# RWKV scan: the decayed state is formed on GpSimd and VectorE instead of by an identity product, and the outputs and the first tile are arranged anew

## What is computed

```
def step(S, inp):                       # S is (heads, 64 values, 64 keys)
    rt, wt, kt, vt, kkt, at = inp
    sa = einsum("bhvk,bhk->bhv", S, -kkt)
    S = S * wt[..., None, :] + sa[..., None] * (kkt * at)[..., None, :] + vt[..., None] * kt[..., None, :]
    return S, einsum("bhvk,bhk->bhv", S, rt)

decay = exp(-exp(-softplus(-lw) - 0.5)) ; a = sigmoid(a0 + (xa @ a1) @ a2)
kk = k * kvec[0] ; kk = kk / max(sqrt(sum(kk * kk)), 1e-12)
k  = k * (1 + (a - 1) * kvec[1])
y  = head_layernorm(y, lnx[0], lnx[1]) ; bonus = sum(r * k * kvec[2]) * v
out = ((y + bonus) * g) @ w_o
```

## Time and profile before

| | us |
|---|---|
| median of 3 runs | 3209.08 (3206.1 to 3211.09) |
| the profiled execution | 3212.0, of which the span of its trace 3210.0 |
| TensorE matmul busy | 3044.9 (95%) |
| VectorE busy | 1132.0 (35%) |
| ScalarE busy | 586.4 (18%) |
| GpSimd busy | 230.5 (7%) |

### The profile page before, as it was taken

One profiled execution on the slowest core, in us unless ns is written; L12 is line 12 of the kernel. 1 busy time (PEld: TensorE's weight loads), 2 busy tenths in 40 slices (PEclk: granted clock), 3 DMA queues, 4 the chain that ended last, 5 costly groups with the idle time before them and its releaser, 6 DMA issues. The chain is left out here.

```text
span 3210.0 us, 54308 instructions
## 1 busy us (share of the span) xinstructions
PE 3044.9 (95%) x24038; PEld 1845.4 (57%) x24038; DVE 1132.0 (35%) x2357; ACT 586.4 (18%) x1323; POOL 230.5 (7%) x202
## 2 busy tenths in 40 slices
PE   7999999899999999989987999999999799998998
PEld 5899884633333333344766444444554687887887
DVE  3455006201100110033065444421231776864650
ACT  1011013300000000022044200000111555442100
POOL 0000000100000000000022100000000323230000
PEclk9999999899999999989988999999999899998999
DMA  9846539489998899932001322333321100005430
GB/s 376 315 173 234 196 142 372 199 355 380 390 372 346 354 380 385 402 125 79 1 2 81 142 106 79 118 131 118 118 76 50 35 15 27 15 3 198 144 144 13
DMA packets 88492, 577.03 MB, mean 180 GB/s; under 512 B 9536, under 2 KB 15936, under 8 KB 20672
## 3 DMA queue, kind: packets, MB, share of 16 engines
q1 hardware_dynamic: 84800, 568.27, 45.3%
q10 hardware_dynamic: 3456, 5.24, 0.4%
HBM read 567.19 MB, written 6.29 MB: 179 GB/s over the span
## 5 line engine op out<-in xcount | busy, mean ns | idle before, releaser
L272 PE MATMUL ps<-H,ring 128*128 128x256 f32 (+1 forms) x2480 | 803.6, 486 | 12.6 <-PEq L3300 4.1
L272 PEld LDWEIGHTS ps<-H,ring 128*128 128x128 f32 x2480 | 477.8, 194 | 336.8 <-issue 296.6
L272 PE MATMUL ps<-W,ring 128*128 128x256 f32 (+1 forms) x1616 | 490.5, 465 | 9.1 <-DVE W L3133 4.1
L1962 PE MATMUL ps<-ring,W 128*32 128x512 f32 (+1 forms) x2816 | 461.4, 594 | 1.7 <-ACT H L2021 1.7
L272 PEld LDWEIGHTS ps<-W,ring 128*128 128x128 f32 x1616 | 307.1, 191 | 192.1 <-issue 166.8
L1962 PEld LDWEIGHTS ps<-ring,W 128*32 128x32 f32 (+1 forms) x2816 | 142.5, 123 | 306.7 <-issue 304.1
L1985 PE MATMUL ps<-ring,W 128*64 128x512 f32 (+1 forms) x1408 | 231.1, 594 | 0.0
L2252 DVE SCALAR_TENSOR_TENSOR W<-ps,vec,W 128x189 f32<-128x189 f32 (+3 forms) x396 | 173.2, 437 | 14.0
L3700 POOL TENSOR_TENSOR ring<-ring 128x512 f32<-128x512 f32 x96 | 131.4, 1388 | 417.6 <-DVE ring L3724 334.7
L1985 PEld LDWEIGHTS ps<-ring,W 128*64 128x64 f32 (+1 forms) x1408 | 70.9, 123 | 156.9 <-issue 156.9
L2070 DVE TENSOR_TENSOR H<-ps,H 128x256 f32<-128x256 f32 x66 | 28.0, 425 | 303.2 <-ACT H L2012 303.2
(11 more groups left out here) (464 smaller groups left out, 3173.4 us busy)
## 6 DMA issues: line engine op xcount, KB each, us to landing
ring<-weights SPq DMA_DIRECT2D x528, 1024.0 KB, 8.0
rkv<-W ACTq DMA_DIRECT2D x16, 256.0 KB, 2.0
ring<-rkv SPq DMA_DIRECT2D x8, 512.0 KB, 3.7
X<-tokens SPq DMA_DIRECT2D x2, 1024.0 KB, 9.0
ring<-rw_tiles SPq DMA_DIRECT2D x8, 256.0 KB, 2.6
rkv<-W ACTq DMA_DIRECT2D x8, 128.0 KB, 5.5
ring<-rkv SPq DMA_DIRECT2D x8, 128.0 KB, 4.0
out<-X SPq DMA_DIRECT2D x8, 128.0 KB, 1.9
```

Of the source, the lines that this page charges most:

```text
L272: mm = pe.matmul(out(o), lhsT=k.ring[:, k.slot(at), p * P:(p + 1) * P], rhs=rhs(kk), start=kk == 0 and not (shared_bank and o % 2), stop=k ...
L1962: mm = pe.matmul(ps[at:at + n, r, :], lhsT=moe.Hg[:, kt, FIRST * e + first:FIRST * e + first + n], rhs=w[e][:, kk * WIDE:(kk + 1) * WIDE], ...
```

## The change

In the recurrence, the identity product is gone. GpSimd forms `kept` = state times decay in SBUF, and VectorE computes product in PSUM times decay plus `kept`, in two instructions (one for each z), where it had one multiplication. The first product into U now starts the accumulation.

```
@@ TensorE, step_a and step_b
                 hat = sc.hat[i % 2]
-                if i < 7:
-                    for z, h in both:
-                        pe.matmul(ps[half(h), sc.U[z], 0:CH], lhsT=k.ident[half(h), half(h)], rhs=hat[half(h), z, :],
-                                  start=True, stop=False, skip_group_check=True)
...
-                                  rhs=sc.Vt[s % 2][rows, b, half(h)], start=i == 0, stop=False, skip_group_check=True)
+                                  rhs=sc.Vt[s % 2][rows, b, half(h)], start=True, stop=False, skip_group_check=True)
@@ GpSimd
+            def kept(s, i):
+
+                if 0 <= s < TILES:
+                    pool.wait_ge(sem["hat"], 7 * s + i)
+                    if i == 1:
+                        pool.wait_ge(sem["exp"], 8 * s + 8)
+                    pool.tensor_tensor(sc.kept[i % 2], sc.hat[i % 2], sc.decay(s, i).unsqueeze(2).to_broadcast([P, 2, CH]),
+                                       ALU.mult).then_inc(sem["kept"], 1)
...
+            for j in range(TILES + 1):
+                s, here = j - 1, inside(j)
+                if here:
+                    masked(j, 0, 0)
+                kept(s, 1)
+                if here:
+                    masked(j, 0, 1)
+                    masked(j, 1, 0)
+                kept(s, 2)
+                if here:
+                    masked(j, 1, 1)
+                    masked(j, 2, 0)
+                    masked(j, 2, 1)
+                for l in range(1, 5):
+                    kept(s, 2 + l)
+                    if here and l < 4:
+                        for z in range(2):
+                            masked(j, 2 + l, z)
@@ VectorE, next_state
-                    a, b = sc.chunk(0, i), 8 + sc.chunk(1, i + 1)
-                    g = sc.G[s % 2][:, a:b + 1:b - a].unsqueeze(2).to_broadcast([P, 2, CH])
-                    dve.tensor_tensor(sc.hat[(i + 1) % 2], ps[:, sc.U[0]:sc.U[1] + 1, 0:CH], g, ALU.mult).then_inc(sem["hat"], 1)
...
+                    dve.wait_ge(sem["kept"], 6 * s + i)
+                    for z in range(2):
+                        ins = dve.scalar_tensor_tensor(sc.hat[(i + 1) % 2][:, z, :], ps[:, sc.U[z], 0:CH], sc.decay(s, i)[:, z:z + 1],
+                                                       sc.kept[i % 2][:, z, :], ALU.mult, ALU.add)
+                    ins.then_inc(sem["hat"], 1)
```

```
@@ VectorE, the turn
                 next_state(s, 0)
-                if inside(q - 1):
-                    gated_output(q - 1)
-                if behind:
-                    dve.wait_ge(sem["mean"], q + 1)
...
                 next_state(s, 2)
                 if here:
                     first_inverse(j, 1)
+                if inside(q - 1):
+                    finished_output(q - 1)
+                if behind:
+                    dve.wait_ge(sem["mean"], q + 1)
...
-                    if behind and l == 5:
-                        scaled_output(q)
```

```
@@ stage_rwkv_project, SyncE
             refill(k, sp, unit_done, 14, ahead=14)
+            sp.wait_ge(k.mm.sem, k.mm.at(out_done[last[1]]))
+            sp.dma_start(first_low(k), k.a["rw_tiles"][0]).then_inc(k.low_in[0], 16)
@@ stage_rwkv
+    LOW_BANK = ((2, 0, 1), (2, 2, 2))
...
                 if i == 0:
-                    pe.wait_ge(tile_in[n % 2], 48 * (n // 2 + 1))
+                    pe.wait_ge(k.low_in[n % 2], 16 * (n // 2 + 1))
...
-                else:
+                elif n:
                     pe.wait_ge(sem["sigmoid"], 3 * n + i)
-                pe.matmul(ps[:, 2, :], lhsT=wj[:, 128 * i:128 * i + 128], rhs=TW if i else TA, start=True, stop=True).then_inc(sem["low"], 1)
+                pe.matmul(ps[:, LOW_BANK[n > 0][i], :], lhsT=wj[:, 128 * i:128 * i + 128], rhs=TW if i else TA, start=True, stop=True).then_inc(sem["low"], 1)
...
+            for z in range(2):
+                scan(0, z)
+            key_to_product(0)
+            unit_keys(0)
+            negative_keys(0)
+            decayed_a(0, 0)
+            bonus(0)
+            decayed_b(0, 0)
```

More of the change, by code:

```diff
@@ L3208, in __init__ @@
         self.BKR = two(lambda: w(1024).rearrange("p (h z i n) -> p h z i n", h=2, z=2, i=2))
-        self.G = two(lambda: w(16))
+        self.wj = [w(512), r(512)]
+        assert self.wj[0].shape == first_low(k).shape and pools["W"][1] == LOW + 512
+        self.G = [k.sm[:, 16 * n:16 * n + 16] for n in range(2)]
         self.sa = two(lambda: w(P))
-        self.hat = two(lambda: w(P).rearrange("p (z v) -> p z v", z=2))
-        self.sq, self.sqd, self.tk = w(512), w(256), k.X[:, 6:8, CTX]
+        self.hat, self.kept = (two(lambda: w(P).rearrange("p (z v) -> p z v", z=2)) for _ in range(2))
+        self.sq, self.sqd, self.tk = r(512), w(256), k.X[:, 6:8, CTX]
         self.g = [*(k.H[:, n, CTX] for n in range(3)), w(S)]
@@ L3533, in state_keys @@
                 mm.then_inc(sem["wt"], 1)
-            for j in range(-1, TILES + 2):
+            for i in range(3):
+                low(0, i)
+            key_squares(0)
+            gate(0)
+            bonus(0)
+            for j in range(TILES + 2):
                 s, q, n = j - 1, j - 2, j + 1
@@ L3689, in _ @@
         def _(pool):
[L3690 to L3701 removed]
+            pool.wait_ge(sem["masks_in"], 16)
```

139 lines of the change are left out of this document (85 added, 54 removed).

## The result

The changed kernel takes 3190.15 us in the median of six runs (3186.36 to 3192.03), the kernel before on the same chip 3208.17. The ratio is 0.9942, with a 95% interval of 0.9929 to 0.9954: 18.6 us by the ratio, 18.0 by the medians. The forecast was 3187.7, in a range of 3174 to 3199.

What follows compares the result with a forecast made beforehand. The prediction took TensorE's stream to bound the scan, with gaps made by another engine. Its terms, -10 - 5.3 - 16.3 + 8.0 + 2.2 = -21.4 us, took the median from 3209.1 to 3187.7 us, range 3174 to 3199.

Steps and rivals of the forecast that it cites:

- C: Outputs leave their places at the tile's end and before the transposes, in tiles 2 to 7: -16.3 us, -13 to -17.
- D: Added GpSimd products, port holds, VectorE half steps and a crowded level 1: +8.0 us, between +3 and +12.
- A: First tile: the first Gram product starts 10.7 us earlier, at 2495.1; counted as -10 us, between -8 and -11.
- B: Identity product gone: -4.5 us at levels 1 to 3 of six tiles, -0.8 past tile 7; together -5.3.
- +2.5 at level 1: Moved outputs overrun VectorE's idle 4.93 us at level 1, meeting GpSimd masks: 0.5 us in each of five tiles.
- the rival in which three do and the wait goes on into the next level: Outputs not hidden at level 1: 6.8 us of VectorE work into 4.93 idle, following level late; 3198 us, chance 0.12.
- three places: Where port holds lie on the path; priced: ahead of the second masking, 3.1 us, and level 4's reciprocal, 2.4 with half steps.
- 0.45 x 7: Hold of VectorE by `kept` ahead of the second masking, 0.45 us in each of seven tiles: 3.1 us.
- E: Last turn but two: outputs between steps 2 and 3, 3.7 us where VectorE idles 1.46: +2.2 us, 0 to +3.
- The slower case: GpSimd's products hold VectorE 1.04 us on the path in all 42 steps: 43.7 us, giving 3226 us; chance 0.04.

Runs made afterwards that it cites:

- the kernel with neither: The changed kernel without the identity product and without `kept`, the new state being product times decay in one instruction: 3182.58 us, 0.9923.
- the best order: The changed kernel with query products before the first masking, old places for the last outputs, bonus factor at level 3: 3180.70 us; with identity product instead of `kept`, 3187.45.

## Why the prediction was right

**The sum** was -21.4 us; the medians say -18.0, the two traces -19.7 for the scan. Every term has its counterpart, but two of them, in C and in D, agree better in size than in place.

**A, the first tile: -10.** Right, step by step. Counted from the issue of the keys, the square was to come after about 4.4 us and came after 4.35, the root was to end after 7.8 and ended after 7.7, and the first Gram product was to start after 15.5 and started after 15.4. The part alone gave 8.3. What the sum lacked is tile 0, 1.3 us longer at the lower clock.

**B, the identity product: -4.5 in the tiles.** Measured between the kernel with and the one without it: -3.4 in the tiles, of 12.5 us of instructions. Levels 1 to 3, where the forecast put the whole gain, give 3.9. Steps 1 and 2 were counted at nothing and cost 0.9. That less than half lies on the path was the right reading.

**C, the outputs: -16.3, with +2.5 at level 1.** Together -13.8 in the tiles; the part alone gave -14.0. That this is so close is in part luck. The rows on which it rested, tile 1's 48.0 and the 1.03 at the tile's end, were the right ones. In tiles 1 to 6 the part gave -14.3, where the forecast had -12.1, because it counted 0.5 for level 1 in each of tiles 3 to 7, and tiles 3 to 6 lose at most 0.1. In tile 7 it gave +0.3, where the forecast had -1.7: there a level takes 5 us and not 7, the outputs aren't hidden, and the lower clock, whose end the forecast counted as a gain, only moved to level 2. In the other tiles level 1 went well: the first addition has no idle time ahead of it, where it had 4.93, and TensorE waits 0.16 and 0.17 us for the transposes behind it. Over the whole scan it waits for these transposes 9.1 us with only the outputs moved and 7.2 before, and tile 7's 1.88 make the difference. The timeline of VectorE there, tile 4 of after:

```profile
2698.25 1.71 DVE L3825 RECIPROCAL W<-W 128x256 f32<-128x256 f32 x1
2700.00 1.55 DVE L3826 SCALAR_TENSOR_TENSOR H<-H,vec,W 128x256 f32<-128x256 f32 x1
2701.59 1.37 DVE L3827 SCALAR_TENSOR_TENSOR H<-H,vec 128x256 f32<-128x256 f32 x1
...
2703.87 0.68 DVE L3905 TENSOR_TENSOR W<-W,ps 128x512 f32<-128x512 f32 x1
```

Two of the five instructions (the two left out, 0.42 each, are the gate's product and `d`) meet a mask, 1.55 and 1.37 where 0.48 is their own time; the rival in which three do and the wait goes on into the next level didn't come, and only in tile 7 does TensorE wait longer for these transposes, 2.22 us.

**D, `kept` and the half steps: +5.5 without level 1.** Measured +6.3 in the tiles, between the kernel with neither and the changed one. The forecast spoke of three places and priced two. Level 4 was right to the hundredth: 0.27 and 0.13 were to make 0.40 us in each of six tiles, and it went from 7.86 to 8.25 or 8.26. The second instruction behind the state there, a maximum with a constant (L3810), takes 0.625 us in the median in place of 0.420, and the half steps give the rest. The second masking came out smaller than the 3.1 forecast: 2.0 on the way to the transposes. "0.45 x 7" rests on `kept` holding the query products, and it lengthens a pair of them by 0.2 us only, since a mask holds them already. Most of the 2.0 falls in tiles 2 and 4, where the first masking, ahead of any `kept` of the turn, waits 1.24 and 1.23 us for the Gram product and not 0.25. The kernel with neither has such waits too, of 0.70 to 0.82 us in tiles 2, 4 and 6, and with them go small gaps of TensorE without a cause in the profile ("issue", 4.9 us in all in the changed kernel, 2.2 with the identity product). What these gaps are, no run here settles. The other 2.1, at levels 1 to 3, had no term here.

```profile
L3810 DVE TENSOR_SCALAR ring<-ring x8: 420/625/627, 2484.4 to 2817.3; 128x512 f32<-128x512 f32 x8
```

**E, the tail: +2.2.** The step was to be near 4 us and took 4.09. By the table of stretches the tail is 1.7 longer, and taking the outputs back gives 0.9 in the trace and 3.5 in the medians, whose intervals overlap. For the whole tail the forecast had +1.4 (with B's -0.8).

**The rivals.** `next_state` was never held: its 96 half instructions take 241 to 285 ns, without one exception:

```profile
L3786 DVE SCALAR_TENSOR_TENSOR W<-ps,sm,W x96: 241/273/285, 2546.8 to 2895.1; 128x64 f32<-128x64 f32 x96
```

The rule of the Trainium skill (SBUF — State Buffer, "SBUF: two separate sides") fits these rows: an instruction that reads PSUM and one SBUF tensor isn't blocked by GpSimd. The page doesn't speak of a column, and the rows say that it doesn't count as a second input. "An instruction with one SBUF input never waits", as the forecast put the rule, is too wide: L3810 has one, and was held. The two half steps together take 0.43 to 0.48 us where one whole instruction took 0.25 to 0.29, so +0.18 or 0.19 where the forecast took 0.13. The slower case needed 1.04 us at each of 42 steps; `kept` and the half steps cost 6.3 us in all 42.

What the forecast didn't see is the condition behind B and D: by the tiles the same edit takes 2.3 us off the kernel before (nothing in the time, within its interval), adds 2.9 beside the two other parts (nothing in the time either), and takes 4.5 off, 6.7 in the time, with the query products and the bonus factor elsewhere. It priced the edit in one order of instructions, and the order was the larger lever.

## What to carry to other kernels

When work leaves the bounding engine, read the idle time of that engine before and after, not only its busy time: where another engine ends last behind the removed work, the busy time turns into waits. It pays where that engine still has idle time, here at levels 1 to 3. A hold on the shared port belonged here to a place and not to an instruction: with the output product taken away, the query products behind it suffered it instead (418 ns in the median before, 957 with the outputs gone), so place short ones where the engine waits for something else. An instruction added to a third engine also shifts what stands behind it in that engine's queue, and that shift can be worth more than the instruction costs; compare stretch by stretch before you name the cause. Time two parts alone before you trust their sum: here the headline part cancelled, and the two parts beside it made the whole gain. A total that agrees can hide two places that don't.

## What the runs showed of the hardware

**The clock in the tail.** Past the last tile the recurrence runs alone, one step in 1.75 us before and 2.00 in the changed kernel. It is not the half steps alone: the windows over such a stretch, before and after, have a granted clock of 1.00 and 0.56.

```profile
2901.00:2912.00 11.00, 8.77 (x232) 7.03 (x233) 2.70 (x8) 2.45 (x9) 0.00 (x0) 1.00 0.89 349
```
```profile
2878.00:2890.00 12.00, 9.26 (x186) 7.76 (x180) 5.58 (x14) 1.54 (x6) 2.01 (x5) 0.56 0.97 391
```

It was low with only the outputs moved too (0.68 in the first 10 us of the tail), and full there with the identity product in the best order. So some of E's 1.7 us is the clock and no wait; how much, no run separates, and the forecast had no term for it.

**A short GpSimd product** of 128x128 takes 0.40 us alone, as the line through the two longer ones said, and up to 1.27 when it comes behind a VectorE scan of 1.23 us: GpSimd, too, can be the one that waits.

**A maximum with a constant from SBUF to SBUF** (`tensor_scalar`), with one tensor operand, is also held by GpSimd (0.63 us against 0.42), where the half steps, with operands from PSUM and SBUF, are not. The Trainium skill (SBUF — State Buffer, "Who interferes with whom") has `tensor_scalar` among the instructions that can take the shared port pair. By that rule, the rows agree.
